# The first norm moved in front of the third modulation tile, and twelve constant loads issued by GpSimd instead of ScalarE

## The reference

```
cond = silu(c)                                   # one vector of 1024
mod  = cond @ ada_w[0] + ada_b[0]                # 1024 x 6144
sh1, sc1, g1, sh2, sc2, g2 = split(mod, 6)
h = rms_norm(x, norm_mix[0]) * (1 + sc1) + sh1   # 256 x 1024
u = h @ even_w_in[0]                             # 1024 x 2976, the first projection
...                                              # attention, MLP, three more layers, a mixture of 8 experts
```

## Time and profile before

| what | value |
|---|---|
| median of 3 runs | 2478.81 us |
| the profiled execution, its own time | 2483.25 us |
| its span in the trace | 2481.9 us |
| TensorE busy | 2364.8 us, 95% |
| VectorE busy | 1789.5 us, 72% |
| ScalarE busy | 1224.3 us, 49% |
| GpSimd busy | 403.5 us, 16% |
| chain that ended last | TensorE 78%, VectorE 11%, DMA 4%, ScalarE 3%, issue 3% |

### The profile page before, as it was taken

How to read it: one execution, slowest core, us unless ns; L and a number is a source line. 1 busy time by engine, 2 the same in 40 slices (tenths; PEclk the granted TensorE clock), 3 DMA queues, 4 the chain that set the end, 5 groups by cost and what they waited for, 6 DMA issues and landing times.

```text
span 2481.9 us, 27398 instructions
## 1 busy us (share of the span) xinstructions
PE 2364.8 (95%) x10947; PEld 1767.8 (71%) x10949; DVE 1789.5 (72%) x2022; ACT 1224.3 (49%) x1441; POOL 403.5 (16%) x446
## 2 busy tenths in 40 slices
PE   6987999999999999899999989999999999999998
PEld 2455898544499875444997558777878778788886
DVE  4756677686688754555665258888888898889897
ACT  1142553223155321223443257676767777777775
POOL 1244470133156010352220000000000000000000
PEclk9998999997999999999999999999999999999999
DMA  7632567541547773104564349989998999899995
GB/s 313 249 152 77 215 261 306 214 187 70 182 184 280 307 302 153 77 34 178 205 261 167 145 158 355 358 326 361 344 366 322 365 344 367 325 364 353 364 351 218
DMA packets 50671, 630.35 MB, mean 254 GB/s; under 512 B 8695, under 2 KB 9384, under 8 KB 12840
## 3 DMA queue, kind: packets, MB, share of 16 engines
q1 hardware_dynamic: 44192, 618.81, 66.0%
q10 hardware_dynamic: 3960, 6.97, 0.8%
q0 software_dynamic: 2384, 2.73, 0.3%
HBM read 624.82 MB, written 3.67 MB: 253 GB/s over the span
## 4 chain that ended last, share of the span: by engine, by line
PE 78%; DVE 11%; DMA 4%; ACT 3%; issue 3%; POOL 0%; ACTq 0%; SPq 0%; DVEq 0%; POOLq 0%
PE psum L1136 17%; PE psum L1137 17%; PE psum L1138 17%; PE psum L1004 5%; PE psum L1031 4%; DVE ring_r L1131 3%; DMA ring<-in_t_moe 3%; PE psum L2500 3%; DVE sbuf L701 2%; PE psum L2494 2%; PE psum L1220 1%; PE psum L741 1%; PE psum L1171 1%; PE psum L3113 1%; DMA ring<-in_t_ada 1%
## 5 line engine op out<-in xcount | busy, mean ns | idle before, releaser
L1137 PE MATMUL psum<-ring_r,sc_r 128*128 128x512 f32 x1688 | 666.3, 395 | 0.0
L1131 DVE TENSOR_TENSOR ring_r<-ring,sbuf_r 128x2048 fp32r<-128x2048 f32 (+1 forms) x287 | 535.8, 1874 | 161.4 <-ACT sbuf_r L1122 160.2
L1122 ACT CAST sbuf_r<-ring 128x2048 fp32r<-128x2048 f32 (+1 forms) x287 | 444.7, 1555 | 331.7 <-PE psum L1138 261.9
L1131 DVE TENSOR_TENSOR ring_r<-ring,sc_r 128x2048 fp32r<-128x2048 f32 (+1 forms) x243 | 477.0, 1974 | 116.2 <-ACT sc_r L1122 115.3
L1122 ACT CAST sc_r<-ring 128x2048 fp32r<-128x2048 f32 (+1 forms) x243 | 397.5, 1643 | 255.2 <-PE psum L1138 218.9
L1136 PE MATMUL psum<-sbuf_r,sc_r 128*128 128x512 f32 (+1 forms) x1148 | 427.0, 372 | 4.0 <-DVE sc L2824 3.4
L1137 PEld LDWEIGHTS psum<-ring_r,sc_r 128*128 128x128 f32 x1688 | 317.6, 188 | 72.3 <-issue 1.4
L701 DVE SCALAR_TENSOR_TENSOR sbuf<-ring,sbuf 128x512 f32<-128x512 f32 x404 | 329.9, 824 | 20.9 <-DMA ring<-in_t_ada 15.6
L1138 PE MATMUL psum<-sbuf_r,sc_r 128*128 128x512 f32 x860 | 340.6, 396 | 0.0
L1136 PE MATMUL psum<-sc_r 128*128 128x512 f32 x828 | 331.3, 400 | 0.0
L1138 PE MATMUL psum<-sc_r 128*128 128x512 f32 x828 | 324.4, 392 | 0.0
(11 more groups left out here) (343 smaller groups left out, 2821.7 us busy)
## 6 DMA issues: line engine op xcount, KB each, us to landing
ring<-in_t_moe SPq DMA_DIRECT2D x168, 2048.0 KB, 7.9
ring<-in_t_ada SPq DMA_DIRECT2D x48, 2048.0 KB, 9.2
ring<-in_t_mlp SPq DMA_DIRECT2D x32, 2048.0 KB, 8.1
ring<-in_t_win SPq DMA_DIRECT2D x17, 2048.0 KB, 9.7
ring<-in_t_ffn SPq DMA_DIRECT2D x16, 2048.0 KB, 8.0
ring<-in_t_out SPq DMA_DIRECT2D x7, 2048.0 KB, 8.6
ring<-in_t_bias SPq DMA_DIRECT2D x2, 2048.0 KB, 10.6
spectra<-sc POOLq DMA_DIRECT2D x5, 512.0 KB, 4.0
```

Of the source, the lines that this page charges most:

```text
L1122: p.act.e.copy(p.r(hi), src).then_inc(*p.sig("high", st.tag, n))
L1131: p.dve.e.tensor_tensor(p.r(src), src, p.r(hi), ALU.subtract).then_inc(*p.sig("lowp", st.tag, n))
L1137: e.matmul(out, l[0], r[1], start=False, stop=False)
```

## The change

Four edits. `DIRECT` gives VectorE five groups of tile 2 instead of four, and TensorE three. The twelve constant loads go from ScalarE's program to GpSimd's, behind the first four seeds. On VectorE the norm moves from behind tile 2 to in front of it. On TensorE the transpose of the small vectors moves in front of the direct products of tile 2 and uses bank 4 instead of bank 1 (bank 1 is now written by the turns), and the turns move from behind the sums of tile 3 to between the direct products of tile 2 and the sums of tile 1. Bank 4 also takes the direct products of tile 3, so these wait for `vecs`.

```
-DIRECT = {1: 4, 2: 4, 3: 4}
+DIRECT = {1: 4, 2: 5, 3: 4}
...
@@ act_begin
-    const(p.INVF, a["k_invf"])
-    const(p.DMASK, a["k_dmask"])
-    const(p.TRI, a["k_tri"])
-    const(p.IOTA, a["k_iota"])
-    for name, w in p.gains.items():
-        const(w, a[name][0].partition_broadcast(128))
     act_gates(p, 4)
+
+
+def pool_constants(p):
+
+    a = p.a
+    for dst, src in [(p.INVF, a["k_invf"]), (p.DMASK, a["k_dmask"]), (p.TRI, a["k_tri"]), (p.IOTA, a["k_iota"])] + [
+            (w, a[name][0].partition_broadcast(128)) for name, w in p.gains.items()]:
+        p.pool.e.dma_start(dst, src).then_inc(*p.land("const"))
...
@@ pool_begin
     pool_seed(p, 4)
+    pool_constants(p)
...
@@ pe_begin
     pe_direct(p, 1)
     pe_sums(p, 1)
+    p.pe.wait_ge(*p.at("posf"))
+    p.pe.e.transpose(p.bank[4][:, 0:128], p.ROWS, p.IDENT).then_inc(*p.sig("vecT"))
     pe_direct(p, 2)
-    p.pe.wait_ge(*p.at("posf"))
-    p.pe.e.transpose(p.bank[1][:, 0:128], p.ROWS, p.IDENT).then_inc(*p.sig("vecT"))
+    pe_modulated(p, 0)
     pe_sums(p, 2)
+    p.pe.wait_ge(*p.at("vecs"))
     pe_direct(p, 3)
     pe_sums(p, 4)
...
@@ dve_begin
-    dve_products(p, 4, 2)
+    dve_products(p, DIRECT[1], 2)
     dve_columns(p, 1)
-    dve_products(p, 4, 3)
     p.dve.wait_ge(*p.at("vecT"))
-    e.tensor_copy(p.VC[:, 24:128], p.bank[1][:, 24:128]).then_inc(*p.sig("vecs"))
+    e.tensor_copy(p.VC[:, 24:128], p.bank[4][:, 24:128]).then_inc(*p.sig("vecs"))
+    dve_norm(p, 0)
+    dve_products(p, DIRECT[2], 3)
     dve_columns(p, 2)
-    dve_norm(p, 0)
-    dve_products(p, 4, 4)
+    dve_products(p, DIRECT[3], 4)
     dve_columns(p, 4)
...
@@ pe_even
-    pe_modulated(p, 0)
```

More of the change, by code:

```diff
@@ L1509, in row @@
         e.dma_start(p.ROWS[r:r + src.shape[0], 0:src.shape[1]], src).then_inc(*p.land("vec"))
-    def const(dst, src):
-        e.dma_start(dst, src).then_inc(*p.land("const"))
     for i, v in enumerate((a["c"][0], a["c_2"][0], a["c_ctx_2"])):
```

## The result

Forecast was a gain of 2.2 us. Measured in 12 runs each: 2484.12 us after the change against 2479.77 us before, ratio 1.0019 with a 95% interval of 1.0010 to 1.0028, that is 2.5 to 6.9 us slower.

A forecast was written before the change was run, and what follows sets the result against it. A relay of waits before TensorE's gapless first projection was taken to bound the start. First matmul at 40.9 instead of 44.94, 4.0 us sooner, less 1.8 for the clock: 2478.8 - 2.2 = 2476.6 us; range 2473.6 to 2479.4.

The forecast's parts named there:

- The landings: Loads at the start: moving the constants shifts weights and x between 0.3 us gained and 1 us lost; 0 taken.
- the landings eat the gain: Rival, chance 0.13: constants in a third queue hold tiles 0 and 1 back 1 to 2 us; gain 0 to 1.
- The issue time: Constant loads: ScalarE loses 17.75 us of issue, free at about 9.6; GpSimd adds 12 x 0.53 = 6.4 us, hidden.
- its queue did not become the wait: Rival, chance 0.06: bias rows behind the constants in GpSimd's queue land late, 10.6 us; slower, 2487.2 us.
- The norm's new place: VectorE: half mean at 24.0, norm 4.95 us to 28.95, columns of tile 2 at 37.35, 1.94 us sooner.
- TensorE hidden: TensorE's new order: fewer products and early turns lie beside VectorE and cost nothing, unless turns came 2 us later.
- The clock: TensorE's projection begins at the lower clock after idling; loss 1.75 to 2.45 us, 1.9 taken, 1.8 in the sum.
- One to one: From the first projection matmul to the kernel's end: a shift of that matmul passes on to the end in full.

The follow-up runs named there:

- e8: Changed kernel with each gain's load reading 128 different rows of a table instead of one row 128 times; one run: tile 2 at 27.02 us, x at 22.09.
- e3: Changed kernel with GpSimd issuing the constants only once the second projection tile has landed; 2478.21 us against 2481.69 for the kernel before, ratio 0.9985.
- e1: Changed kernel with its twelve constant loads back on ScalarE; 2480.96 us against 2481.69 for the kernel before, ratio 0.9992.
- e4: Changed kernel with late constants on GpSimd plus three matmuls nothing reads in TensorE's pauses; ratio 0.9957 to the kernel before, in seven runs.
- e9: Kernel before with only the constants moved to GpSimd, issued when the second projection tile has landed; ratio 0.9997 to the kernel before.
- e10: The kernel of e4 measured again on another chip; 2477.11 us against 2479.91 for the kernel before, ratio 0.9990.
- e7: Changed kernel with the twelve constant loads issued by SyncE behind x and ahead of tile 2; one run: tile 2 at 33.89 us, x at 19.48.

## Why the prediction was wrong

**The landings.** The step that failed is the cost of the constant loads: "The bytes are the same as before and the transfers start 1.7 us sooner on another queue", with a loss of at most 1 us and 0 taken. Measured in the changed kernel: tile 1 late by 1.75 us, tile 2 by 6.9, x by 7.1. The rival "the landings eat the gain" named the mechanism, but had it at 1 to 2 us, with a gain of 0 to 1 left. I priced loads by bytes and by their issuer; e8 shows that most of the price (5.7 of the 8.3 us between no early constants and all of them) lies in what they read.

The traces also show why nothing of it was seen before. Through ScalarE the twelve loads were some 1728 packets (q10 has 3960 in the whole program before and 2232 after), through GpSimd some 432 (q0 2384 and 2816), so a packet of GpSimd's carries four times as much. The Trainium skill states in "DMA: Bandwidth & Descriptors", section "Queues, rings and completion order", that an engine takes turns between its queues packet by packet. The traces agree: before, from 32 to 48 us, q1 and q10 had 456 packets each, and after, from 19 to 25 us, q1 had 160 and q0 165. What a turn costs is the difference. Before, those 456 small packets took 3.3% of the engines' time beside 97.7% for the weights, and the whole ran at 426 GB/s; after, the 165 large ones took 76.5%, beside 33.4% for the weights, at 138 GB/s. So ScalarE's constants trickled until 53.4 us and held nobody up but ScalarE; GpSimd's were through at 28.0, ahead of tile 2. That the same reads did no harm while spread is measured there; that it is the spreading alone, and not also the packets' size or the kind of queue, was not isolated.

The rows gave no clear sign of it. The 31.8 us for 32 KB and the issue of 4.27 us were a gain's, and the mask of 384 KB had gone in 0.46, but on that queue a table of 64 KB (k_iota) took 22.1 us to land as well.

**The issue time.** Right: ScalarE was free at 10.0. GpSimd took 0.53 us for each load, as the earlier trace rows said, and its queue did not become the wait: the seeds were in time. But moving them was needed only to get them out of ScalarE's way, and that needed no early issue (e3).

**The norm's new place.** Right in each term (e3), once x is there. In the changed kernel the half mean came at 28.55 instead of 24.0, and the relay from there took 5.32 us instead of 4.95: the half mean now followed the first square at once, so that the second square came to lie between it and the root.

**TensorE hidden.** Wrong as a consequence: from a tile 2 at 32.74, 4.31 us for six products (the clock had fallen while TensorE waited), then turns, sums and the products of tile 3 came one behind another to 43.26, and VectorE waited for it. I had said that this would begin with turns 2 us late; they began 8.6 us later than the 28.4 of the prediction, at 37.0.

**The clock.** Right in kind, short in size. The projection began at the lower level and lost 2.96 us instead of 1.8 in the changed kernel, 2.21 in e3 and 1.43 in e1. That the loss is the clock's is shown by e4: with the pauses filled it is 0. The prediction's own working gave 1.9 and its sum used 1.8; the difference is nothing beside the rest. My bounds of 1.75 to 2.45 came from two rises; the traces taken since have anything from 0.7 (e9) to 3.0.

**One to one.** Only roughly right: at the entry of the experts the starts' differences stand again to within 2.6 us, and for the filled pauses only 70% (e4) and half (e10) of them. That the result came out so close to its start (4.4 of 5.1) is no proof of the step. Over the whole, runs of the kernel before alone lie between 2473.8 and 2484.8 us. From three runs 1.2 us apart I took its median for sharper than it is.

## What to carry to other kernels

A load moved to another queue is another load: ask what it overtakes there, in how large packets, and where it reads. Constants that nobody needs for 30 us go behind the loads that the start waits for, by a wait on one of these. And where a burst on TensorE follows a relay of waits, a few matmuls that nothing reads can be worth more than they take (here three for 2.6 us of the start, of which no gain in the whole is shown).

## What the runs showed of the hardware that was not expected

- Broadcasting one row of 256 or 384 bytes to 128 partitions straight from DRAM is slow when such loads run close together: eight of them with four tables took 7.5 us of all sixteen DMA engines, with different source rows 2.3 us (31.2% and 9.5% of 24 us). The gains came in at 30 GB/s in the changed kernel (19 to 25 us) and at 29 in e7; that is no fixed ceiling, since ScalarE's queue before moved 0.11 MB in the 2 us from 49.6. In e7 the whole rate fell to between 8 and 52 GB/s for 4.8 us.
- GpSimd's twelve loads made about 432 packets where ScalarE's made about 1728.
- Two queues with work had the same number of packets, 456 and 456 in 16 us before, 160 and 165 in 6 us after, whatever the packets' size.
- An issue behind queued loads can hold its engine: ScalarE up to 5.19 us for one, SyncE 5.58 us in e7. GpSimd's issues of the same loads never took over 0.59 us.
